# Bias rows copied to DRAM 32 instead of 128 times, read back in four parts, and all loads that are no weights issued by ScalarE or GpSimd

## The chip, the cores and the metric

One core of one Trainium2 chip. The time is the device time of the whole kernel in microseconds (us), the median of several executions.

## What is computed

Two residual networks one after the other, 256 latent tokens (and 256 context tokens) of width 1024, all in float32. `first_block` has four layers, each with an adaLN modulation from `c @ w_ada`: window GQA, MLA, mLSTM, and again a GQA layer. `second_block` takes its result and mixes three branches: NSA heads (a), sliding window heads (b) and forgetting attention (c), then a gated convolutional FFN. What matters here is the relative bias of the a and b heads:

```python
dist = n_prev * Q_BLOCK + qi - ki
bias = jnp.transpose(tab[t5_bucket(dist)], (2, 3, 0, 1))[:, :, None]
logits = jnp.einsum('bgrnqd,bgnkd->bgrnqk', qb, kb).astype(jnp.float32) * (HEAD_DIM ** -0.5) + bias
```

A bias depends on the distance of query and key only. For each head it is one row of 383 values, and a tile of 128 queries by 256 keys needs that row shifted by one for each query.

## The kernel before, in words

Every weight matrix is streamed through a ring of six slots (`w_raw`, NR = 6) of up to 128x1024 float32, 512 KB. SyncE (SP) issues the load of block j + 6 when TensorE has used block j (`w_load`, L3559 to L3564). ScalarE (ACT) rounds a block to its high part (`w_round`, `w_h`), VectorE (DVE) takes the rest (`w_rest`, `w_l`), three blocks ahead of TensorE as a rule, and TensorE does each product in three passes. Every engine takes its instructions strictly in the order in which one shared program emits them; the helper lines L2206 (matmul), L2513 (ACT copy) and L2826 (DVE tensor_tensor) stand for most of them. A `fence` is the newest mark of every engine at that point of the program; whoever waits for it waits for all of them.

All loads that are no weights were also issued by SP in the kernel before, in the same queue as the weight blocks: `gate_load` (a row of gains, one per layer of the first block, L3566), `ml_tables` (L3571), `mix_tables` (six small tables, L3577), `mix_diag` and `mix_bias` (L3589, L3593), `mix_causal` (L3598), `fg_neg` (L3603) and `cp_load` (L3610).

The bias tiles are made in the last layer of the first block (`layer_gqa(3)`, L727 on), by steps of a generator, `Mixers.tables`, placed between its projections. TensorE multiplies a one-hot table with the 32 buckets (`mix_vec_mm`), DVE copies the 8 rows of 384 values to the tile `vec` (`mix_vec`), and `mix_diag` writes `vec` 128 times to a DRAM scratch `[128, 8, 384]`. Both kinds, b and then a, use the one tile `vec`:

```python
    def mix_vec(p, m, b, k):
        p.wait_ge(("mix", "vec_mm", k), ("d_diag", "b") if k == "a" else None)
        p.copy(m.vec[:], p.n.ps[0:8, b, 0:384]).then_inc(*p.mark("mix", "vec", k))
```

Later `mix_bias` reads the scratch back with a row step of one element less than a copy, so that partition p gets the row shifted by p: `BT` `[128, 8, 256]`, 1 MB. BTb is read at the fence in the middle of `layer_gqa(3)`, BTa at the beginning of the b heads' attention.

`layer_gqa` runs the projections q(0) and z(0) (each four blocks and more), then the first attention interleaved with q(1) and z(1), then the second attention interleaved with `ada`, the modulation of the next layer. An attention unit goes PE scores, DVE peak, ACT exponential, DVE scale, PE transpose, ACT copy, PE values.

`fg_neg` writes the forget gate's row to DRAM, waits for that and reads it back as a tile for all partitions; it is emitted between the norms of the c heads' keys, whose power -0.5 runs on GpSimd (POOL, `norm_total`, L3499).

Of the kernel before, what the change touches and what calls it, by code (L numbers as in the profile page):

```python
# [16 lines left out]
D = 1024  # L17
# [153 lines left out]
CONST_AT = {}  # L171
# [56 lines left out]
class Net:  # L228
# [25 lines left out]
    def new(self, name, shape, dt=F32):  # L254
        return self.at(name, shape, dt, self.here(4 * int(np.prod(shape[1:]))))
# [92 lines left out]
def drain(gen):  # L348
    for _ in gen:
        pass  # L350


def weave(main, other, num, den):

    owed = 0
    for _ in main:
        owed += num
        while owed >= den:
            owed -= den
            next(other, None)  # L360
    drain(other)
# [20 lines left out]
def chain(*gens):  # L382
    for g in gens:
        yield from g
# [26 lines left out]
class Steps:  # L411
# [4 lines left out]
    name = None  # L416
# [29 lines left out]
        self.n.value[key] = self.newest = (sem, self.count[key[0]])  # L446
        return sem, 1

    def landed(self, name, *which):

        sem = self.n.sem("_".join([name, *map(str, which)]))
        self.n.value[(name, *which)] = (sem, 16)
        return sem, 16

    def fence(self):
# [10 lines left out]
    gate_load = gate_split = gate_spread = idle  # L466
# [6 lines left out]
    ml_tables = ml_gate_in = ml_sig = ml_scans = ml_ends = ml_max = ml_cols_turn = ml_cols = ml_last_mm = ml_last = idle  # L473
# [3 lines left out]
    mix_tables = mix_gains = mix_vec_mm = mix_vec = mix_diag = mix_bias = norm_in = norm_total = norm_scale = idle  # L477
    mix_dup = mix_key_turn = mix_key_out = mix_v = mix_gz = mix_pos0 = mix_pos_in = mix_pos = mix_causal = idle
    fg_turn = fg_bias = fg_exp = fg_min = fg_scan = fg_neg = fg_col = fg_tanh = fg_gate = idle
    cp_load = cp_hid = cp_hs = cp_turn = cp_g0 = cp_g1 = cp_kv = cp_sq = cp_vc = cp_rs = cp_k = cp_kT = cp_l0 = cp_logits = idle  # L480
# [246 lines left out]
    def layer_gqa(p, i, base, hT, m, mix=None):  # L727

        f = p.fence()
        tables = mix.tables(f) if mix else iter(())  # L730
        next(tables, None)
        drain(m.q(0, hT, f))
        next(tables, None)
        drain(m.z(0, hT, f))
        next(tables, None)
        m.flush()
        p.dense = PAIR
        att = m.attention(0, (0, 1), m.Pt[0], m.PT[0], f, 3, 2)
        steps = 2 * len(m.units(0))
        weave(att, chain(m.q(1, hT, f), m.z(1, hT, f)), 8 * len(m.tiles), steps)  # L740
        m.flush()
        f = p.fence()
        p.stage_tok = [f, f]
        if mix:
            mix.bias("b", f)
        gate, post = p.ends(i, base, 97 if i == 3 else 0, len(m.tiles))
        groups = [(i, 4), (i, 5)] + ([(i + 1, b) for b in range(4)] if i < 3 else [])
        att = m.attention(1, (2, 3), m.Pt[1], m.PT[1], f, 4, 3)
        weave(att, p.ada(PAIR, groups, Gate(p, i, *gate, f), range(5), lag=3), 4 * len(groups) + 2, steps)
        p.dense = DENSE  # L750
        post.free = p.fence()
        return post
# [185 lines left out]
class Weights:  # L938
# [6 lines left out]
    def next(self, name, i, ks, cols, raw=False, ahead=AHEAD):  # L945
        n, b = self.p.n, Block()
        b.j, b.name, b.i, b.words = len(self.order), name, i, ks * cols
        b.is_raw, b.free = raw, None
        b.nsplit = self.split_n
        if not raw:  # L950
            self.split_n += 1
        self.order.append(b)
        s = b.j % NR
        view = lambda t: t[:, 0:ks * cols].rearrange("p (k n) -> p k n", k=ks)
        b.raw, b.h, b.l = view(n.w_raw[s]), view(n.w_h[s]), view(n.w_l[s])
        b.ready = [("loaded", b.j)] if raw else [("w_rounded", b.nsplit), ("w_rest", b.nsplit)]
        self.p.w_load(b.j + NR)
        self.split_to(b.j + ahead, b.j + max(ahead - 1, 0))
        return b
# [849 lines left out]
class Mixers(Later):  # L1809
    def __init__(self, p, base):  # L1810
        n = p.n
# [39 lines left out]
        self.gb, self.tab = new("gains", [128, 6, 64], 1792), new("tab", [33, 16], 3328)  # L1851
        self.oh = {"a": new("oha", [33, 384], 3392), "b": new("ohb", [33, 384], 4928)}
        self.vec = new("vec", [8, 384], 6464)
        self.scr = {k: n.scratch(f"m_bias{k}", (128, 8, 384)) for k in "ba"}
        self.fscr = n.scratch("m_c", (8, 256))
        self.hm, self.sel4, self.row31 = sm[:, 16:24], sm[:, 24:56], sm[:, 56:57]
        self.gz = sm[:, 96:160].rearrange("p (t c) -> p t c", t=2)
# [5 lines left out]
    def tables(self, fence):  # L1863

        p = self.p
        p.mix_tables(self, fence)
        yield
        p.mix_gains(self)
        for x, k in ((1, "b"), (0, "a")):
            b = p.take(TRANS)  # L1870
            p.mix_vec_mm(self, b, x, k)
            p.mix_vec(self, b, k)
            p.give(b, ("mix", "vec", k))
            p.mix_diag(self, k)
            yield

    def bias(self, kind, fence):
        self.p.mix_bias(self, kind, fence)
# [321 lines left out]
class Tensor(Steps):  # L2200


    name = "pe"
# [302 lines left out]
class Scalar(Steps):  # L2506


    name = "act"

    def f(p, out, a, func, bias=0.0, scale=1.0, accum=None):
# [211 lines left out]
    def norm_total(p, m, key, x, nh, a, qs_free, tmp, fence):  # L2723
        p.wait_ge(a, qs_free, fence)
        p.f(m.sq[x][:, 0:nh * 64], m.kn[x][:, 0:nh * 64], ACT.Square).then_inc(*p.mark("norm", "sq", *key))
# [89 lines left out]
    def ff_high(p, m, k):  # L2815
        p.wait_ge(("ffn", "ft", k), m.f)
        p.copy(m.ff.h[:, k, :], m.ft[k % 4][:]).then_inc(*p.mark("ffn", "high", k))


class Vector(Steps):  # L2820


    name = "dve"
# [398 lines left out]
    def mix_tables(p, m, fence):  # L3222
        p.wait_ge(fence)
        p.e.memset(m.tab[32:33, :], NEG).then_inc(*p.mark("mix", "tab"))
# [76 lines left out]
    def fg_neg(p, m, fence):  # L3301
        p.wait_ge(("forget", "c"))
        p.ts(m.f[0][:], m.f[3][:], -1.0, ALU.mult).then_inc(*p.mark("forget", "nc"))
# [42 lines left out]
    def cp_rs(p, m):  # L3346
        st = m.small[0:32, 176:178]
        p.wait_ge(("comp", "sq"))
        p.ts(st[:, 1:2], st[:, 0:1], 1.0 / 64, ALU.mult, EPS, ALU.add).then_inc(*p.mark("comp", "mean"))
# [142 lines left out]
class Pool(Steps):  # L3492


    name = "pool"

    def power(p, out, key, tok):
# [26 lines left out]

    def norm_total(p, m, key, x, nh, a, qs_free, tmp, fence):
        p.power(m.small[:, 64 + 16 * x + 8:64 + 16 * x + 8 + nh], ("norm", "rstd", *key), ("norm", "mean", *key))

    def cp_rs(p, m):
        p.power(m.small[0:32, 177:178], ("comp", "rstd"), ("comp", "mean"))
# [7 lines left out]
class Sync(Steps):  # L3537


    name = "sp"  # L3540
# [18 lines left out]
    def w_load(p, j):  # L3559
        n, s = p.n, j % NR  # L3560
        if j < len(n.order):
            b = n.order[j]
            p.wait_ge(n.order[j - NR].free if j >= NR else None)
            p.e.dma_start(n.w_raw[s][:, 0:b.words], n.w[b.name][b.i]).then_inc(n.sem(f"w_dma{s}"), 16)  # L3564

    def gate_load(p, gate, free):  # L3566
        src = p.n.dram[f"l{gate.i}_g_post"].unsqueeze(0).to_broadcast([128, D])
        p.wait_ge(free)
        p.e.dma_start(gate.gpost[:], src).then_inc(*p.landed("d_gpost", gate.i))

    def ml_tables(p, m, fence):  # L3571
        p.wait_ge(fence)
        for k in ("scan_mul", "scan_add"):
            o = CONST_AT[k][0]
            p.e.dma_start(m.rows[k][:], p.n.dram["cst"][0:64, o:o + 512]).then_inc(*p.landed("d_scan", k))

    def mix_tables(p, m, fence):  # L3577
        n, o = p.n, CONST_AT["hm"][0]
        p.wait_ge(fence)
        p.e.dma_start(m.gb[:].rearrange("p a d -> p (a d)"), n.dram["qk_gain_2"].rearrange("l a d -> l (a d)").to_broadcast(  # L3580
            [128, 384])).then_inc(*p.landed("d_gb"))
        p.e.dma_start(m.small[:, 0:8], n.dram["sinks_2"].to_broadcast([128, 8])).then_inc(*p.landed("d_sinks"))
        p.e.dma_start(m.small[:, 16:57], n.dram["cst"][:, o:o + 41]).then_inc(*p.landed("d_hm"))
        p.e.dma_start(m.tab[0:32, :], n.dram["rel_bias_2"]).then_inc(*p.landed("d_tab"))
        for k, name in (("a", "oh_nsa"), ("b", "oh_swa")):
            o = CONST_AT[name][0]
            p.e.dma_start(m.oh[k][:], n.dram["cst"][0:33, o:o + 384]).then_inc(*p.landed("d_oh", k))

    def mix_diag(p, m, k):  # L3589
        p.wait_ge(("mix", "vec", k))  # L3590
        p.e.dma_start(m.scr[k].rearrange("p h m -> h p m"), m.vec[:].unsqueeze(1).to_broadcast([8, 128, 384])).then_inc(*p.landed("d_diag", k))

    def mix_bias(p, m, k, fence):  # L3593
        src = bass.AP(tensor=m.scr[k].tensor, offset=127, ap=[[8 * 384 - 1, 128], [384, 8], [1, 256]])
        p.wait_ge(("d_diag", k), fence)
        p.e.dma_start(m.BT[k][:], src).then_inc(*p.landed("d_bias", k))

    def mix_causal(p, m, fence):  # L3598
        o = CONST_AT["causal"][0]
        p.wait_ge(fence)  # L3600
        p.e.dma_start(m.causal[:], p.n.dram["cst"][:, o:o + 256]).then_inc(*p.landed("d_causal"))

    def fg_neg(p, m, fence):  # L3603
        p.wait_ge(("forget", "nc"))
        p.e.dma_start(m.fscr, m.f[0][:]).then_inc(*p.landed("d_c"))
        p.wait_ge(("d_c",), fence)
        p.e.dma_start(m.cbc[:].rearrange("p h t -> p (h t)"), m.fscr.rearrange("h t -> (h t)").unsqueeze(0).to_broadcast(
            [128, 2048])).then_inc(*p.landed("d_cbc"))

    def cp_load(p, m, fence):  # L3610
        p.wait_ge(fence)
        p.e.dma_start(m.w2[:], p.n.dram["cmp_w2_2"].rearrange("l w (c p) d -> p (l w) c d", p=128)).then_inc(*p.landed("d_w2"))

    def program(p):
        Steps.program(p)
# [70 lines left out]
```

## Time and profile before

| | us |
|---|---|
| median of three runs | 1620.43 |
| the three runs | 1619.82, 1620.43, 1622.74 |
| the profiled execution | 1617.48 |
| its span, first to last instruction | 1615.7 |
| mean granted TensorE clock over the span | 0.975 |
| busy: PE, DVE, ACT, POOL | 1487.1, 1002.2, 768.4, 67.1 |
| HBM written | 4.20 MB |

The profile is of one execution. Its span is 1.8 us shorter than its time. DMA rows give a transfer by its two tensors, and "SPq" or "ACTq" for the queue that issued it; times are us from the span's start. TensorE's busy time is modelled from its pipelined instructions. The clock is a share of full speed (2.4 GHz): 0.50 is 1.2 GHz.

### The profile page before, as it was taken

The page shows a single profiled execution, that of the slowest core. Times are in us where ns is not written, and L with a number is a line of the kernel's source. Part 1 is how long each engine was busy: PE and PEld are TensorE (multiplying, and loading weights), DVE is VectorE, ACT ScalarE, POOL GpSimd, SP SyncE. Part 2 cuts the span into 40 slices and gives each one's busy share as a digit, 9 for nine tenths or more (in the row PEclk, how much of TensorE's full clock was granted, in tenths as well). Part 3 has the DMA queues.
Part 4 walks back from the last instruction along what each step waited for, and adds up shares of the span by engine and source line. Part 5 has one row for each costly group of instructions (what it writes and reads, how often), then busy time and mean ns, then how long its engine had stood idle before and what let it go on. Part 6 is the DMA issues. An engine that isn't in the chain of part 4 may idle for free.

```text
span 1615.7 us, 24203 instructions
## 1 busy us (share of the span) xinstructions
PE 1487.1 (92%) x9392; PEld 1209.8 (75%) x9392; DVE 1002.2 (62%) x2306; ACT 768.4 (48%) x1642; POOL 67.1 (4%) x74
## 2 busy tenths in 40 slices
PE   6999998999999999999979954988899999989999
PEld 4777756777778787888757743766788889889987
DVE  3547676565566657536585634685776658677763
ACT  4336575453654534321243513574666537455542
POOL 0000000100000100010010000000200110000000
PEclk9999999999999999999989987999899999999999
DMA  9131172321551332211642265233445463345553
GB/s 350 53 105 53 53 260 67 99 91 53 176 190 40 105 111 79 91 53 52 222 157 78 87 119 102 86 124 111 157 143 183 135 221 105 133 157 193 184 190 136
DMA packets 61554, 206.25 MB, mean 128 GB/s; under 512 B 7602, under 2 KB 12412, under 8 KB 61312
## 3 DMA queue, kind: packets, MB, share of 16 engines
q1 hardware_dynamic: 60136, 203.13, 37.9%
q8 instruction: 75, 1.23, 0.3%
q10 hardware_dynamic: 1304, 1.57, 0.3%
q14 instruction: 39, 0.32, 0.1%
HBM read 200.47 MB, written 4.20 MB: 127 GB/s over the span
## 4 chain that ended last, share of the span: by engine, by line
PE 70%; DVE 14%; DMA 7%; ACT 5%; issue 3%; POOL 1%; SPq 0%; POOLq 0%; ACTq 0%; DVEq 0%
PE ps L2206 65%; PE ps L2209 5%; DVE w_l L2826 3%; DMA w_raw<-in_l_q 2%; DMA w_raw<-in_l_z 2%; DMA w_raw<-in_l_out 1%; DVE st L2922 1%; ACT w_h L2513 1%; DVE x L2834 1%; ACT l_P L2516 1%; DVE l_h_lat L2834 1%; DMA w_l_ada<-in_l_ada 1%; DVE m_P L3406 1%; DVE l_P L2830 1%; DVE l_xn L2830 1%
## 5 line engine op out<-in xcount | busy, mean ns | idle before, releaser
L2826 DVE TENSOR_TENSOR w_l<-w_raw,w_h 128x1024 fp32r<-128x1024 f32 (+3 forms) x265 | 316.9, 1206 | 74.5 <-ACT w_h L2513 74.0
L2513 ACT ACTIVATE w_h<-w_raw 128x1024 fp32r<-128x1024 f32 (+3 forms) x265 | 273.3, 1042 | 152.7 <-DMA w_raw<-in_l_q 30.4
L2206 PE MATMUL ps<-w_h,l_hTh 128*128 128x512 f32 (+1 forms) x384 | 157.5, 410 | 0.6 <-DVE w_l L2826 0.5
L2206 PE MATMUL ps<-w_l,l_hTh 128*128 128x512 f32 (+1 forms) x384 | 152.9, 398 | 0.0
L2206 PE MATMUL ps<-w_h,l_hTl 128*128 128x512 f32 (+1 forms) x384 | 152.9, 398 | 0.0
L2516 ACT ACTIVATE l_P<-ps,st 128x512 f32<-128x512 f32 (+1 forms) x128 | 77.6, 608 | 79.6 <-DVE st L2834 52.2
L2206 PE MATMUL ps<-f_hTh,w_h 128*128 128x256 f32 x352 | 99.0, 281 | 0.0
L2206 PE MATMUL ps<-f_hTl,w_h 128*128 128x256 f32 x352 | 98.8, 281 | 0.0
L2206 PE MATMUL ps<-f_hTh,w_l 128*128 128x256 f32 x352 | 98.7, 280 | 0.0
L2206 PE MATMUL ps<-l_hTh,w_h 128*128 128x512 f32 (+1 forms) x264 | 97.4, 369 | 0.5 <-issue 0.5
L2922 DVE TENSOR_REDUCE st<-ps 128x1 f32<-128x512 f32 (+2 forms) x112 | 72.7, 649 | 39.9 <-PE ps L2206 39.4
L2206 PE MATMUL ps<-l_hTl,w_h 128*128 128x512 f32 (+1 forms) x264 | 96.9, 367 | 0.0
L2206 PE MATMUL ps<-l_hTh,w_l 128*128 128x512 f32 (+1 forms) x264 | 96.8, 367 | 0.0
L2206 PEld LDWEIGHTS ps<-w_h,l_hTl 128*128 128x128 f32 x384 | 73.4, 191 | 16.9
L2206 PEld LDWEIGHTS ps<-w_h,l_hTh 128*128 128x128 f32 x384 | 73.6, 192 | 15.6 <-issue 1.4
L2206 PEld LDWEIGHTS ps<-w_l,l_hTh 128*128 128x128 f32 x384 | 73.7, 192 | 14.7
L2206 PE MATMUL ps<-l_PT,l_V 128*64 128x128 f32 (+1 forms) x712 | 70.1, 282 | 3.1 <-DVE l_ogf L2834 3.1
L2206 PEld LDWEIGHTS ps<-l_PT,l_V 128*64 128x64 f32 (+1 forms) x712 | 55.7, 151 | 21.5 <-issue 13.6
L2209 PE MATMUL ps<-cst,l_P 128*128 128x128 f32 x416 | 66.9, 281 | 4.4 <-ACT l_PT L2513 1.7
L2206 PE MATMUL ps<-m_hTh,w_h 128*128 128x256 f32 x224 | 64.8, 290 | 4.1 <-issue 1.3
L2206 PEld LDWEIGHTS ps<-f_hTh,w_h 128*128 128x128 f32 x352 | 66.8, 190 | 0.2 <-issue 0.2
L2206 PEld LDWEIGHTS ps<-f_hTl,w_h 128*128 128x128 f32 x352 | 66.9, 190 | 0.0
(441 smaller groups left out, 3503.1 us busy)
## 6 DMA issues: line engine op xcount, KB each, us to landing
w_raw<-in_l_ada SPq DMA_DIRECT2D x81, 512.0 KB, 4.3
w_raw<-in_l_z SPq DMA_DIRECT2D x32, 512.0 KB, 3.6
w_raw<-in_l_out SPq DMA_DIRECT2D x32, 512.0 KB, 3.6
w_raw<-in_m_merge SPq DMA_DIRECT2D x24, 512.0 KB, 3.3
w_raw<-in_f_gate SPq DMA_DIRECT2D x22, 512.0 KB, 3.2
w_raw<-in_f_up SPq DMA_DIRECT2D x22, 512.0 KB, 3.3
w_raw<-in_f_down SPq DMA_DIRECT2D x22, 512.0 KB, 4.2
w_raw<-in_l_q SPq DMA_DIRECT2D x16, 512.0 KB, 4.6
```

The lines of the kernel that those rows point to most:

```text
L2206: return p.e.matmul(out, lhsT, rhs, start=start, stop=stop)
L2209: return p.e.transpose(out, a, ident)
L2513: return p.e.activation(out, a, func, scale=scale)
L2516: return p.e.activation(out, a, func, bias=bias, scale=scale, accum_out=accum)
L2826: return p.e.tensor_tensor(out, a, b, op)
L2830: return p.e.tensor_scalar(out, a, s1, None, op0)
L2834: return p.e.scalar_tensor_tensor(out, a, s, b, op0, op1)
L2922: p.e.reduce_max(soft.stat(u, 0, nh), ps if nh == 1 else ps.rearrange("p (h k) -> p h k", h=nh), AX.X).then_inc(*p.mark(*soft.key("peak", u)))
L3406: v = p.e.tensor_tensor_reduce(dst, src, bias[i], 1.0, -3.0e38, ALU.add, ALU.max, mx[:, i:i + 1])
```

## The change

The scratch holds 32 copies of the rows in place of 128. `mix_bias` reads it in four loads of 32 partitions each, with the offset lowered by 32 elements per part; they share one semaphore, which is waited for at 64. `gate_load`, `ml_tables`, `mix_tables`, `mix_diag`, `mix_bias`, `mix_causal` and `cp_load` go, otherwise unchanged, from the class of SP to that of ACT, `fg_neg` to that of POOL. In `Mixers.tables` the `yield` stands ahead of `mix_diag` and not behind it, and `layer_gqa` takes one step more from it, so that each copy is issued one step later: copy b after z(0), directly ahead of `mix_vec("a")`, and copy a right behind the flush that follows.

```diff
-    def landed(self, name, *which):
+    def landed(self, name, *which, of=1):
         sem = self.n.sem("_".join([name, *map(str, which)]))
-        self.n.value[(name, *which)] = (sem, 16)
+        self.n.value[(name, *which)] = (sem, 16 * of)
         return sem, 16
...
         next(tables, None)
         m.flush()
+        next(tables, None)
         p.dense = PAIR
...
-        self.scr = {k: n.scratch(f"m_bias{k}", (128, 8, 384)) for k in "ba"}
+        self.scr = {k: n.scratch(f"m_bias{k}", (32, 8, 384)) for k in "ba"}
...
             p.give(b, ("mix", "vec", k))
+            yield
             p.mix_diag(self, k)
-            yield
...
 class Scalar(Steps):
...
+    def gate_load(p, gate, free):
...
+    def ml_tables(p, m, fence):
...
+    def mix_tables(p, m, fence):
...
+    def mix_diag(p, m, k):
+        p.wait_ge(("mix", "vec", k))
+        p.e.dma_start(m.scr[k].rearrange("p h m -> h p m"), m.vec[:].unsqueeze(1).to_broadcast([8, 32, 384])).then_inc(*p.landed("d_diag", k))
+
+    def mix_bias(p, m, k, fence):
+        p.wait_ge(("d_diag", k), fence)
+        for r in range(4):
+            src = bass.AP(tensor=m.scr[k].tensor, offset=127 - 32 * r, ap=[[8 * 384 - 1, 32], [384, 8], [1, 256]])
+            p.e.dma_start(m.BT[k][32 * r:32 * r + 32], src).then_inc(*p.landed("d_bias", k, of=4))
+
+    def mix_causal(p, m, fence):
...
+    def cp_load(p, m, fence):
...
 class Pool(Steps):
...
+    def fg_neg(p, m, fence):
+        p.wait_ge(("forget", "nc"))
+        p.e.dma_start(m.fscr, m.f[0][:]).then_inc(*p.landed("d_c"))
+        p.wait_ge(("d_c",), fence)
+        p.e.dma_start(m.cbc[:].rearrange("p h t -> p (h t)"), m.fscr.rearrange("h t -> (h t)").unsqueeze(0).to_broadcast(
+            [128, 2048])).then_inc(*p.landed("d_cbc"))
...
 class Sync(Steps):
...
-    def mix_diag(p, m, k):
-        p.wait_ge(("mix", "vec", k))
-        p.e.dma_start(m.scr[k].rearrange("p h m -> h p m"), m.vec[:].unsqueeze(1).to_broadcast([8, 128, 384])).then_inc(*p.landed("d_diag", k))
-
-    def mix_bias(p, m, k, fence):
-        src = bass.AP(tensor=m.scr[k].tensor, offset=127, ap=[[8 * 384 - 1, 128], [384, 8], [1, 256]])
-        p.wait_ge(("d_diag", k), fence)
-        p.e.dma_start(m.BT[k][:], src).then_inc(*p.landed("d_bias", k))
```

The other functions are taken out of `Sync` in the same words in which they stand in `Scalar` and `Pool`.

## Rows read from the trace of the kernel before

**Rows 1.** The page: busy us (share of the span) xinstructions.
```profile
PE 1487.1 (92%) x9392; PEld 1209.8 (75%) x9392; DVE 1002.2 (62%) x2306; ACT 768.4 (48%) x1642; POOL 67.1 (4%) x74
```

**Rows 2.** The chain that ended last, by time: start us, us, what.
```profile
...
937.26 33.62 DMA w_raw<-in_l_q
974.80 3.95 PE ps L2206 x9
...
979.19 1.99 PE ps L2206 x9
...
983.63 23.65 DMA w_raw<-in_l_z
```

**Rows 3.** Timeline of SP: start us, us, queue, line, transfer (count).
```profile
936.86 0.31 SPq L3591 DMA_DIRECT2D m_biasb<-m_vec  x1
937.26 13.00 SPq L3564 DMA_DIRECT2D w_raw<-in_l_q  x2
...
973.18 0.30 SPq L3591 DMA_DIRECT2D m_biasa<-m_vec  x1
```

**Rows 4.** Windows: stretch, length, busy us of five engines, TensorE clock, DMA share, GB/s.
```profile
937.00:969.00 32.00, 14.29 (x102) 12.15 (x101) 5.79 (x8) 3.65 (x6) 0.00 (x0) 0.78 0.56 83
969.00:973.00 4.00, 0.00 (x0) 0.00 (x0) 0.73 (x2) 1.33 (x2) 0.00 (x0) 0.50 0.52 208
```

**Rows 5.** Timeline of PE: start us, us, operation, idle before and releaser.
```profile
946.09 0.28 PE L2206 MATMUL ps<-l_hTh,w_l 128*128 128x256 f32 x1
...
974.80 0.80 PE L2206 MATMUL ps<-l_kTh,l_qT 128*128 128x512 f32 x1 [23.52 <-ACT l_P L2516]
...
1008.89 0.75 PE L2209 MATMUL ps<-identr,l_qs 128*128 128x128 f32 x4 [17.57 <-ACT l_PTs L2513]
```

**Rows 6.** Timelines of ACT (four lines) and DVE (one), same columns.
```profile
943.61 0.39 ACT L2515 ACTIVATE l_zT<-ps 128x256 f32<-128x256 f32 x1 [1.47 <-PE ps L2206]
...
970.91 1.06 ACT L2513 ACTIVATE w_h<-w_raw 128x1024 fp32r<-128x1024 f32 x1 [26.91 <-DMA w_raw<-in_l_q]
...
991.24 0.28 ACT L2515 ACTIVATE st<-st,l_sink 128x1 f32<-128x1 f32 x1
1007.30 1.06 ACT L2513 ACTIVATE w_h<-w_raw 128x1024 fp32r<-128x1024 f32 x1 [15.78 <-DMA w_raw<-in_l_z]
...
972.61 0.54 DVE L2837 COPY m_vec<-ps 8x384 f32<-8x384 f32 x1
```

**Rows 7.** The page, DMA issues: count, KB, median us from issue to landing.
```profile
w_raw<-in_l_z SPq DMA_DIRECT2D x32, 512.0 KB, 3.6
```

**Rows 8.** Timeline of all engines at the start of layer_gqa(3).
```profile
922.61 1.04 ACT L2513 ACTIVATE w_h<-w_raw 128x1024 fp32r<-128x1024 f32 x1
922.73 0.69 DVE L2826 TENSOR_TENSOR l_qs<-l_ropeA,l_qs 128x512 fp32r<-128x512 f32 x1 [1.02 <-ACT l_qs L2513]
...
923.49 0.33 SPq L3580 DMA_DIRECT2D m_gains<-in_qk_gain  x1
```

**Rows 9.** Timelines of SP (two lines) and ACT at the second attention's start.
```profile
1046.32 0.38 SPq L3596 DMA_DIRECT2D m_BTb<-m_biasb  x1
1046.74 0.58 SPq L3569 DMA_DIRECT2D l_gpost<-in_l_g_post  x1
...
1047.06 0.69 ACT L2516 ACTIVATE l_P<-ps,st 128x512 f32<-128x512 f32 x1 [1.16 <-DVE st L2834]
```

**Rows 10.** Timelines of SP, POOL, DVE and PE around the forget gate.
```profile
1160.70 0.30 SPq L3605 DMA_DIRECT2D m_c<-m_f  x1
1162.01 0.33 SPq L3607 DMA_DIRECT2D m_cbc<-m_c  x1
...
1161.63 2.54 POOL L3499 TENSOR_TENSOR m_small<-m_small,phalf 128x8 f32<-128x8 f32 x1 [6.09 <-DVE m_small L2831]
...
1167.36 1.23 DVE L2826 TENSOR_TENSOR m_qsl<-m_kn,m_qsl 128x1024 fp32r<-128x1024 f32 x1
...
1172.51 0.81 PE L2209 MATMUL ps<-identr,m_qsl 128*128 128x128 f32 x8
```

More of the change, by code:

```diff
@@ L2817, in ff_high @@
         p.copy(m.ff.h[:, k, :], m.ft[k % 4][:]).then_inc(*p.mark("ffn", "high", k))
+    def gate_load(p, gate, free):
+        src = p.n.dram[f"l{gate.i}_g_post"].unsqueeze(0).to_broadcast([128, D])
+        p.wait_ge(free)
+        p.e.dma_start(gate.gpost[:], src).then_inc(*p.landed("d_gpost", gate.i))
+    def ml_tables(p, m, fence):
+        p.wait_ge(fence)
+        for k in ("scan_mul", "scan_add"):
+            o = CONST_AT[k][0]
+            p.e.dma_start(m.rows[k][:], p.n.dram["cst"][0:64, o:o + 512]).then_inc(*p.landed("d_scan", k))
+    def mix_tables(p, m, fence):
+        n, o = p.n, CONST_AT["hm"][0]
+        p.wait_ge(fence)
+        p.e.dma_start(m.gb[:].rearrange("p a d -> p (a d)"), n.dram["qk_gain_2"].rearrange("l a d -> l (a d)").to_broadcast(
+            [128, 384])).then_inc(*p.landed("d_gb"))
+        p.e.dma_start(m.small[:, 0:8], n.dram["sinks_2"].to_broadcast([128, 8])).then_inc(*p.landed("d_sinks"))
+        p.e.dma_start(m.small[:, 16:57], n.dram["cst"][:, o:o + 41]).then_inc(*p.landed("d_hm"))
+        p.e.dma_start(m.tab[0:32, :], n.dram["rel_bias_2"]).then_inc(*p.landed("d_tab"))
+        for k, name in (("a", "oh_nsa"), ("b", "oh_swa")):
+            o = CONST_AT[name][0]
+            p.e.dma_start(m.oh[k][:], n.dram["cst"][0:33, o:o + 384]).then_inc(*p.landed("d_oh", k))
+    def mix_diag(p, m, k):
[7 more added lines that the diff above has]
+    def mix_causal(p, m, fence):
+        o = CONST_AT["causal"][0]
+        p.wait_ge(fence)
+        p.e.dma_start(m.causal[:], p.n.dram["cst"][:, o:o + 256]).then_inc(*p.landed("d_causal"))
+    def cp_load(p, m, fence):
+        p.wait_ge(fence)
+        p.e.dma_start(m.w2[:], p.n.dram["cmp_w2_2"].rearrange("l w (c p) d -> p (l w) c d", p=128)).then_inc(*p.landed("d_w2"))
 class Vector(Steps):
@@ L3564, in w_load @@
             p.e.dma_start(n.w_raw[s][:, 0:b.words], n.w[b.name][b.i]).then_inc(n.sem(f"w_dma{s}"), 16)
[L3566 to L3587, printed above, removed]
@@ L3589, in mix_diag @@
-    def mix_diag(p, m, k):
-        p.wait_ge(("mix", "vec", k))
-        p.e.dma_start(m.scr[k].rearrange("p h m -> h p m"), m.vec[:].unsqueeze(1).to_broadcast([8, 128, 384])).then_inc(*p.landed("d_diag", k))
-    def mix_bias(p, m, k, fence):
-        src = bass.AP(tensor=m.scr[k].tensor, offset=127, ap=[[8 * 384 - 1, 128], [384, 8], [1, 256]])
-        p.wait_ge(("d_diag", k), fence)
-        p.e.dma_start(m.BT[k][:], src).then_inc(*p.landed("d_bias", k))
[L3598 to L3612, printed above, removed]
```

## The prediction

> **What bounds the kernel now.** I read the page first. TensorE is busy for 92% of the span [rows 1], so only the 8% in which it stands still can be won by moving transfers. The chain of waits in order of time shows where: two of its DMA pieces, in the last attention layer, stand far above the landing time of a block (3.6 us [rows 7]): 33.62 and 23.65 us [rows 2]. Both are loads of a weight block, and both were issued behind a copy of a bias row to DRAM: m_biasb at 936.86, m_biasa at 973.18 [rows 3]. The reader should see three things there.
>
> First, the copy is slow and wide in time, not in bytes. From 937 to 969 the windows show 83 GB/s at a DMA share of 0.56, with weight blocks in between; in the window behind it the blocks left over run at 208 GB/s at a share of 0.52 [rows 4]. So the copy ends at about 969, and a block that needs 3.6 us elsewhere [rows 7] needs 33.6 behind it. Second, TensorE pays for it with 23.52 and 17.57 us of idleness [rows 5], after which it runs at half clock: nine matmuls take 3.95 us, and a little later 1.99 [rows 2]. Third, who is late. ACT waited 26.91 and 15.78 us for the blocks, because it takes its work in order [rows 6]. DVE is late for a second reason: mix_vec("a") overwrites the tile that copy b reads, so it waits until copy b has landed, and it runs at 972.61, just behind the end of copy b [rows 6].
>
> **The change, part by part.** The sum is made against the profiled execution, 1617.48 us, 2.95 below the median of the three runs (1620.43); I take the difference over to the median.
>
> **1. Copies a quarter as long.** The scratch shrinks from 128 to 32 copies, from 1.57 to 0.39 MB each. The outermost dimension stays the 8 heads, so I take the same rate: 969.0 less 937.9 (issue plus about 1 us) is 31.1 us, a quarter of it 7.8. Issue and completion: a block of 512 KB lands in 3.6 us [rows 7], of which its 256 KB on half of the engines at 208 GB/s [rows 4] are 1.3; the other 2.3 I add. A copy alone then takes 10.1 us. Bounds: 3.6, a whole block's landing, if the rate was set by something that the size removes; 34 us, as now, if it doesn't shrink.
>
> **2. Copy b is issued later and loses its cover.** The moved yield puts mix_diag("b") behind all of z(0), directly ahead of mix_vec("a"), which waits for it. Before, the whole of z(0) lay between. Now: z(0)'s last matmul starts at 946.09 [rows 5], its evacuation on ACT takes 0.39 [rows 6], so ACT issues copy b at 946.8. It lands at 946.8 + 10.1 + 1.3 (one weight block shares its engines) = 958.2. Until then DVE stands, and with it the softmax, then TensorE. Behind mix_vec now come 974.80 less 972.61, 2.2 us, until TensorE resumes [rows 5, 6]. It resumes at 960.4 in place of 974.80: **14.4 us won**, not 23.5. Queued behind the wait on DVE are the first reductions and w_l blocks; ACT waits in mix_diag("a") for the same moment, which costs nothing more, as its softmax needs DVE first.
>
> **3. Copy a.** It starts at about 959 and is over at 970. The block that ended the second stall was issued 8.8 us after TensorE resumed (983.63 less 974.80 [rows 2]); now that is 969, and on another queue. So it lands in 3.6 us, before ACT wants it: ACT's step at 1007.30 moves to the end of the one before it, 991.24 + 0.28 = 991.5 [rows 6]: 15.8 us. Without that stall the half clock behind it goes as well, 3.95 less 1.99 = 2.0 [rows 2]. **17.8 us won.** The half clock behind the first stall stays, since TensorE still stands for 9 us.
>
> **4. The six loads of mix_tables on ACT.** SP issued them from 923.49 on, when DVE's l_qs of 922.73 to 923.42 had met the fence [rows 8]. In ACT's order they stand ahead of the rounding now at 922.61. That waits for the fence (0.8) and six issues of 0.33 to 0.43, so it slips by 3.4 us. ACT can catch up later, but DVE's rest of that block stands ahead of the rope of q. I take 2.0 lost (bounds 0 and 3.4).
>
> **5. BTb in four parts and gpost on ACT.** SP issued one load and gpost at 1046.32 and 1046.74, 0.38 and 0.58 us [rows 9]; ACT now issues 4 x 0.38 + 0.58 = 2.1 us from 1046.3 on, and its softmax, on the chain at 1047.06 [rows 9], starts at 1048.4: 1.3 lost (bounds 0 and 2.1). The data are read only in the b heads' attention, a stage later. BTa's four parts (1.5 us by the same 0.38) come while TensorE works through projections that don't need ACT's softmax: nothing, 1.5 without that cover.
>
> **6. fg_neg on POOL.** POOL waits for the forget row, issues m_c, waits for it, issues m_cbc; SP's issues stood at 1160.70 and 1162.01. The power of ck's second tile, at 1161.63 for 2.54 us, is behind them now. DVE's m_qsl ends at 1168.6 and TensorE wants it at 1172.51 [rows 10]: 3.9 us of slack. No row has a DMA issued by POOL. Lower bound SP's 0.3 us each, upper bound that power's 2.54 each: the power ends 1 to 7 us later. I take 0.3 lost (bounds 0 and 3).
>
> **7. The rest** (gpost of layers 0 to 2, scan tables, causal mask, w2): one or two issues of 0.3 to 0.6 us each, in gaps where ACT waits for the same fence or for TensorE. 0.4 lost (0 and 2). SP loses its waits for the bias rows; no block was due in them.
>
> Sum: 14.4 + 17.8 - 2.0 - 1.3 - 0.3 - 0.4 = **28.2 us won**: 1589.3 for the profiled execution, **1592.2** for the median.
>
> **Rivals.** *Copies don't shrink with their bytes.* For: 49 GB/s (1.57 MB in 32 us) is far under what the same engines do, so the limit isn't known. If a copy takes 20 us, DVE stands 10 longer: 1602. Against: the rate is steady over the whole stretch.
>
> *The later copy b turns the gain round.* This is the slower side: DVE's wait for copy b at about 947 is uncovered, each microsecond of it counts. It eats all 28.2 when copy b takes 11.4 + 28.2 = 39.6 us from its issue; at 45 us the time is 1626. This needs a copy that stays at 31 us and is slowed by a third by weights that now interleave with it. Against: the quarter size.
>
> *POOL's issues are slow.* A POOL operation on 128x8 takes 2.54 us beside a busy DVE [rows 10]. At the upper bound TensorE waits 3 us more at 1172, and with the upper bounds of 4 and 5 the time is 1598. The Trainium skill, SBUF — State Buffer, section "SBUF: two separate sides", says that VectorE and GpSimd share a port pair under an exclusive lock, so that descriptors of a DMA issued from GpSimd can wait for a VectorE instruction. By that rule the move to POOL is the wrong way round for this load, and the 3 us are due; no row here shows a DMA of POOL, so the trace neither confirms nor denies it.
>
> *Copy b is short.* If it needs 3.6 us, TensorE hardly stops, and the half clock goes too: 7 and 2 us more, less part of the costs: 1584.
>
> **Chances.** Forecast 0.68; copies shrink less 0.12; POOL and ACT dear 0.10; copy b short 0.07; slower 0.03. A measurement of this kernel can tell about 0.2%, 3.2 us, from no change; only the slow case comes near it (0.01 of "same" is its near edge). The range takes in the short copy and the 20 us copy: 1584 to 1603.
>
> **What would show it.** Right: no DMA piece over 6 us in the chain between 937 and 1010; HBM written falls by 2.4 MB; one idleness of TensorE of 8 to 11 us ended by DVE behind m_vec, at half clock after it; none of 17 us; four loads of BTb on ACTq, softmax behind them about 1.3 us late. Wrong: TensorE's idleness before the softmax over 15 us or under 4; a weight block behind copy a that takes over 8 us; a gap of TensorE at ck's transposes; ACT's roundings at the start of the layer later by more than 4 us.

## The result, and the profile after

| | before | after | ratio, 95% interval |
|---|---|---|---|
| median, us (range) | 1620.12 (1619.43 to 1622.74) | **1596.38** (1592.49 to 1598.45) | 0.9849 [0.9831, 0.9867] |
| profiled execution, us; its span | 1617.48; 1615.7 | 1595.08; 1593.3 | |
| mean granted clock of TensorE in it | 0.975 | 0.981 | |

The change wins 23.7 us, where 28.2 had been worked out; the time lies inside the predicted range (1584 to 1603), 4.2 us above the forecast of 1592.2. The same kernel, timed again beside the experiments, gave 1599.05. The page of the kernel after: the time TensorE is busy, and what the copies write.

```profile
PE 1492.8 (94%) x9392; PEld 1212.9 (76%) x9392; DVE 1002.5 (63%) x2306; ACT 768.8 (48%) x1642; POOL 67.7 (4%) x76
...
HBM read 200.47 MB, written 1.84 MB: 127 GB/s over the span
```

The instructions are the same 9392 matmuls as in [rows 1]; HBM writes fell from 4.20 MB to 1.84, by twice the 1.18 MB that a copy has lost. The chain of waits of after, in order of time, answers to [rows 2]:

```profile
927.96 1.07 ACT w_h L2515
929.05 1.23 DVE w_l L2870
...
934.40 0.85 PE ps L2210 x8
935.25 9.71 PE ps L2207 x44
944.96 0.65 PE ps L2210 x8
945.61 7.09 PE ps L2207 x60
952.73 9.35 DMA m_biasb<-m_vec
...
964.38 4.02 PE ps L2207 x9
...
969.25 2.45 PE ps L2207 x9
...
983.52 0.64 PE ps L2210 x4
984.16 3.88 PE ps L2207 x22
```

Both pieces of a weight block (33.62 and 23.65 us) are gone. In their place stands one new piece, the copy b itself: the kernel no longer waits for weights behind a copy, it waits for the copy. The windows show what the clock did around it (stretch, length, busy us of PE, PEld, DVE, ACT and POOL, TensorE's granted clock, DMA share, GB/s):

```profile
936.00:943.00 7.00, 7.00 (x27) 4.97 (x26) 4.56 (x9) 1.69 (x2) 0.00 (x0) 0.51 0.31 110
943.00:957.00 14.00, 14.00 (x104) 12.32 (x103) 5.78 (x8) 4.99 (x8) 0.00 (x0) 1.00 0.50 160
957.00:964.00 7.00, 0.58 (x3) 0.14 (x1) 1.79 (x4) 0.45 (x1) 0.00 (x0) 0.70 0.33 44
964.00:974.00 10.00, 9.62 (x36) 7.31 (x37) 8.74 (x21) 7.59 (x18) 0.00 (x0) 0.69 0.34 39
974.00:984.00 10.00, 8.18 (x59) 6.09 (x57) 8.14 (x23) 5.89 (x16) 0.00 (x0) 0.99 0.46 157
984.00:988.00 4.00, 4.00 (x25) 2.79 (x23) 2.57 (x6) 2.26 (x5) 0.00 (x0) 0.60 0.08 10
```

The row of 957 to 964 is the stall; the first, the fourth and the last are stretches at half clock (1.2 GHz), wholly or partly. Before, TensorE had a clock of 1.00 from 925 to 940. The timeline has the three idle times of PE in front of them (three rows), and DVE's row names the copy as what held the first softmax back; [rows 5, 6] are the rows of before:

```profile
934.40 0.85 PE L2210 MATMUL ps<-identr,l_qs 128*128 128x128 f32 x8 [1.74 <-DVE l_qs L2870]
964.38 0.79 PE L2207 MATMUL ps<-l_kTh,l_qT 128*128 128x512 f32 x1 [6.79 <-ACT l_P L2518]
983.52 0.64 PE L2210 MATMUL ps<-identr,l_qs 128*128 128x128 f32 x4 [1.67 <-ACT l_PTs L2515]
962.18 0.55 DVE L2881 COPY m_vec<-ps 8x384 f32<-8x384 f32 x1 [8.61 <-DMA m_biasb<-m_vec]
```

Now the first 1.74. ACT's timeline at the start of layer_gqa(3) has the six table loads between two roundings:

```profile
923.88 0.61 ACT L2515 ACTIVATE l_qs<-l_ropeA 128x512 fp32r<-128x512 f32 x1
925.30 0.33 ACTq L2835 DMA_DIRECT2D m_gains<-in_qk_gain  x1
...
927.54 0.37 ACTq L2842 DMA_DIRECT2D m_ohb<-in_cst  x1
927.96 2.01 ACT L2515 ACTIVATE w_h<-w_raw 128x1024 fp32r<-128x1024 f32 x2 [3.47 <-issue]
```

To see where time is won and lost I took the start of the same ACT instruction in both traces and subtracted. The kernel after comes into the last attention layer 1.8 us late, stands 6.3 us late behind the tables, 10.4 early behind the first softmax, 9.5 early ahead of the place of the old second stall, 25.3 behind it, 22.9 behind the start of the second attention, and 22.4 early at the end. The first 1.8 is a drift that differs from run to run (the repeat of the same kernel has 0.8 at that point).

### The profile page after: what moved, and what is told of

Read it like the earlier page. It is cut to its first block, busy times and chain, and to the rows that moved or that the text cites. A ratio compares the mean times of both kernels' runs of the same rounds, so it can differ in the third digit from the quotient of the medians.

```text
span 1593.3 us, 24198 instructions
## 1 busy us (share of the span) xinstructions
PE 1492.8 (94%) x9392; PEld 1212.9 (76%) x9392; DVE 1002.5 (63%) x2306; ACT 768.8 (48%) x1642; POOL 67.7 (4%) x76
## 3 DMA queue, kind: packets, MB, share of 16 engines
HBM read 200.47 MB, written 1.84 MB: 127 GB/s over the span
## 4 chain that ended last, share of the span: by engine, by line
PE 73%; DVE 14%; ACT 5%; DMA 4%; issue 3%; POOL 1%; ACTq 0%; SPq 0%; POOLq 0%; DVEq 0%
PE ps L2207 67%; PE ps L2210 5%; DVE w_l L2870 3%; DVE st L2966 1%; DMA w_raw<-in_l_out 1%; DVE x L2878 1%; ACT l_P L2518 1%; ACT w_h L2515 1%; DMA w_l_ada<-in_l_ada 1%; DVE l_h_lat L2878 1%; DMA m_biasb<-m_vec 1%; DVE l_xn L2874 1%; DVE l_P L2874 1%; DMA w_raw<-in_m_aq 1%; POOL mstat L3544 0%
## 5 line engine op out<-in xcount | busy, mean ns | idle before, releaser
L2207 PEld LDWEIGHTS ps<-w_l,l_hTh 128*128 128x128 f32 x384 | 73.5, 192 | 14.8
```

Of the source, the lines that this page charges most:

```text
L2207: return p.e.matmul(out, lhsT, rhs, start=start, stop=stop)
```

## The experiments

All were timed against the kernel before, which was timed again with each of the three batches (1620.27, 1620.99 and 1620.74). The ratios carry an interval of about 0.2 to 0.25%, 3 to 4 us, so small steps are read from the traces. A trace shows one execution only: differences between two traces that lie away from the edited place are scatter, and they reach several us. The "distance" given below is how far the same ACT instruction starts behind (+) the fastest kernel found (32 copies, all on SP but the two copies themselves).

### First batch: size alone, and two parts undone

**The kernel after again** gives the reference for the others.

> The changed kernel once more, as the measure for the others of this set. Both theories: 1596, within 0.2%.

1599.05 us, ratio 0.987 [0.9848, 0.9891]. The trace repeats that of after row for row: chain piece of copy b 9.36 us, TensorE's half clock at 935 and at 984.

**Size alone**, the kernel before with

```
-        self.scr = {k: n.scratch(f"m_bias{k}", (128, 8, 384)) for k in "ba"}
+        self.scr = {k: n.scratch(f"m_bias{k}", (32, 8, 384)) for k in "ba"}
...
-        ... m.vec[:].unsqueeze(1).to_broadcast([8, 128, 384])
+        ... m.vec[:].unsqueeze(1).to_broadcast([8, 32, 384])
```

and the four reads, every transfer and the yield where they were.

> The kernel before with 32 copies and four reads, everything still issued by SP and at its old place. Theory (the length of the copies is the whole gain, the move of the queue only costs): copy b lands at about 947, ahead of mix_vec a, and the weight blocks behind either copy are at most 8 us late, most of which the blocks in hand cover; both idle times of TensorE go and no load is added to ACT: 1580 to 1584. Rival (the weight blocks must leave the copies' queue): blocks behind each copy still stall TensorE for 5 to 8 us each, so that it is no faster than the changed kernel: 1592 to 1598.

**1581.98 us**, ratio 0.9766 [0.9747, 0.9786]. The theory held: size alone wins 38 us, and the rest of the change costs 14 to 17 (1596.38 or 1599.05 less 1581.98). The four reads came in with the smaller size, but the first of them is issued at 1011.35, behind both places where TensorE had stood, so they can't be what removed these stalls. The timelines of SP and DVE in this kernel show why nothing waits for the row: DVE writes it again at 953.94, 12.1 us behind the issue of copy b and without a wait, with the whole of z(0) between them.

```profile
941.85 0.31 SPq L3591 DMA_DIRECT2D m_biasb<-m_vec  x1
942.24 3.92 SPq L3564 DMA_DIRECT2D w_raw<-in_l_q  x2
948.55 3.13 SPq L3564 DMA_DIRECT2D w_raw<-in_l_z  x2
954.51 0.30 SPq L3591 DMA_DIRECT2D m_biasa<-m_vec  x1
...
953.94 0.54 DVE L2837 COPY m_vec<-ps 8x384 f32<-8x384 f32 x1
```

**mix_tables back on SP**, otherwise the kernel after.

```
 class Scalar(Steps):
-    def mix_tables(p, m, fence):
...
 class Sync(Steps):
+    def mix_tables(p, m, fence):
```

> The changed kernel with mix_tables back on SP. Theory (the six issues on ACT delay the rounding and DVE's rest, TensorE waits 1.7 us and then runs 7 us at half clock, 4.5 us in all): 1592, and no idle time of TensorE ahead of the transposes of q. Rival (the 4.5 us are covered later, or are scatter of the two profiled executions): 1596.

1588.77 us, ratio 0.982 [0.9793, 0.9847]: 7.6 to 10.3 us better than after by the medians, more than expected, with five runs from 1585.67 to 1594.51. Copy b's piece is still 9.37 us and TensorE still stands 6.79. What is gone is the half clock ahead of it, a part of that behind it, and all of it at the place that follows (22 matmuls in 2.49 us against 3.88). The windows of this kernel:

```profile
925.00:940.00 15.00, 14.58 (x92) 12.21 (x93) 12.96 (x21) 6.23 (x9) 0.00 (x0) 1.00 0.59 192
...
958.00:968.00 10.00, 10.00 (x44) 7.69 (x45) 9.57 (x24) 8.34 (x19) 0.00 (x0) 0.83 0.35 43
...
976.00:980.00 4.00, 3.93 (x33) 3.06 (x34) 3.10 (x8) 2.90 (x8) 0.00 (x0) 1.00 0.15 40
```

Behind the same stall of 6.79 us the next ten microseconds have a clock of 0.83 here and 0.69 in the kernel after. In the traces the kernel after loses 4.7 us against this one ahead of the copy, about 1 behind the stall and about 1.5 at the 22 matmuls, some 7 in all. The 1.5 can't be put down to the tables: other kernels below have the half clock at that place with the tables on SP.

**The yield back**, otherwise the kernel after.

```
             p.give(b, ("mix", "vec", k))
+            p.mix_diag(self, k)
             yield
-            p.mix_diag(self, k)
```

and the extra `next(tables, None)` out.

> The changed kernel with the yield behind mix_diag again and one step less in layer_gqa: copy b is issued by ACT right behind mix_vec b, ahead of z(0). Theory (the wait of mix_vec a for the later copy b is what is left of the first stall): copy b is issued at about 941, lands at 951, mix_vec a waits for at most 1 us, TensorE loses neither the 7 us nor the half clock behind them: 1587. Rival (ACT's wait for mix_vec b, or the copy beside the blocks of z, takes it back): 1594 to 1598.

1583.72 us, ratio 0.9772 [0.9751, 0.9793]: 12.7 to 15.3 better than after by the medians, 10.1 by the two traces. Here ACT issues copy b at 940.94 and copy a at 954.32. The 9.4 us of the copy lie inside these 13.4, and TensorE has one idle time over 1 us from 936 to 975, 1.68 at its end.

### Second batch: the queue alone, the yield alone

**128 copies in the kernel after**, the first line of the size edit taken back.

> The changed kernel with 128 copies of each row again (the four reads take the first 32): queue moves and later copies, without the smaller size. Theory (the later copy b is paid for by its whole length): copy b goes out at about 953 as in the changed kernel, lasts about 32 to 34 us, the second DVE write of the row waits for it, so PE stands some 23 us longer there than in the changed kernel, and nothing waits behind copy a: 1616 to 1630, no better than the kernel before. Rival (the second rival of the prediction, that queue moves win the second stall and the late copy costs nothing): about 1602.

1630.18 us, ratio 1.0056 [1.0034, 1.0078]: slower than before, and just above the theory's range; the rival (1602) fell. The theory was right on the first stall (23.7 us longer than in the kernel after) and wrong in that nothing would wait behind copy a. TensorE's timeline:

```profile
991.38 0.79 PE L2207 MATMUL ps<-l_kTh,l_qT 128*128 128x512 f32 x1 [30.50 <-ACT l_P L2518]
...
1020.58 0.75 PE L2210 MATMUL ps<-identr,l_qs 128*128 128x128 f32 x4 [11.77 <-ACT l_PTs L2515]
```

The first stall is longer than the 23.52 of [rows 5], because the copy starts later; the second is still there, shorter than the 17.57 of before, though copy and weights stand in two queues.

**The two copies alone to ACT**, 128 of them, in the kernel before (mix_diag moved from Sync to Scalar).

> The kernel before with the two copies of 128 rows issued by ACT instead of SP, nothing else. Theory (both stalls of before come from the length of the copy, the first by the row buffer, the second by the queue): the weight loads no longer stand behind the copies, PE's first idleness shrinks to what the buffer alone asks (copy b out at about 937 to 941, done 32 us later, 14 to 20 us idle instead of 23.5), the second of 17.6 us is gone: 1594 to 1604. Rival (the copies hold the weight loads back by using the same DMA engines, in whatever queue): both stalls stay, 1612 to 1622.

1613.68 us, ratio 0.9947 [0.9928, 0.9966]: my theory (1594 to 1604) failed, and the time lies in the rival's range. Three rows of its chain:

```profile
939.93 34.32 DMA m_biasb<-m_vec
...
985.95 17.82 DMA w_raw<-in_l_z
1006.13 3.72 PE ps L2206 x22
```

A block needs 17.82 us on SP's queue while a copy runs from ACT's. So a long copy slows the weights whatever queue it is in. The queue isn't without effect at this length: the block issued right behind copy b lands after 17.14 us here and after 33.62 in one queue with it, and TensorE's second idleness is 11.73 us in place of 17.57. But the first stays at 21.94 (23.52 before), since DVE's second write still waits for the copy itself. The queue by itself is worth about 7 us of the 38 (5.5 to 11.7 by the interval of the ratio).

**The yield alone**: size alone, as above, with the yield moved and the extra `next(tables, None)`, all on SP.

> The best one so far (kernel before with 32 copies and four reads, all issued by SP) with the yield moved ahead of the copy and the one more step of the tables, as in the changed kernel. Theory (it is the moved yield that delays copy b by some 12 us, whichever engine issues it): copy b goes out at about 950 to 955, the second write of the row waits for it, PE stands 5 to 8 us and gets the half clock after: 1589 to 1597. Rival (the delay came from ACT's order of work, not from the yield): 1580 to 1584.

1586.14 us, ratio 0.9778 [0.9755, 0.98]: between the two by its median, and 4.2 us above size alone, which the intervals don't tell apart. The trace decides for the theory's mechanism: copy b goes out at 954.72, 10.4 us behind its row (944.3), the second write waits 9.0 us for it, and TensorE's timeline has

```profile
966.41 0.80 PE L2207 MATMUL ps<-l_kTh,l_qT 128*128 128x512 f32 x1 [7.18 <-ACT l_P L2517]
```

The distance grows from 7.0 ahead of this place to 14.8 behind it, 7.8 us. So it is the yield that delays the copy, on either engine. How much of the 7.8 us the whole time keeps on SP is less sure: the execution in the trace is the slowest of the five (1591.53).

**The copies alone to ACT**, 32 of them, at their old places.

> Kernel before with 32 copies and four reads, the two copies alone issued by ACT at their old places, everything else by SP. Theory (with copies of 9.4 us the queue they stand in hardly matters): the weight block no longer waits 10 us behind copy b, ACT is held back once by up to 1 us: 1578 to 1583, within 2 us of the same with SP. Rival (ACT's place in the queue costs by itself, because ACT waits for the row before it can go on): 1584 or more.

**1579.38 us**, ratio 0.9748 [0.9726, 0.9771], the fastest found, though not told apart from 1581.98. The reason I gave was wrong. I had expected the weight block not to wait behind copy b; its chain has

```profile
937.70 9.99 DMA w_raw<-in_l_q
```

and with the copy on SP's queue the same piece is 9.98 us. For copies of this length the queue makes no difference to the weights.

### Third batch: the other parts, one at a time on the fastest kernel

**Six table loads to ACT.**

> The best one so far (kernel before, 32 copies, four reads, the two copies alone on ACT) plus the six table loads of layer_gqa(3) on ACT: part 4 of the prediction by itself. Theory (they push ACT's rounding of a weight back, PE stands 1.7 us and then has the half clock for some 7 us): slower than the best one by 3 to 5 us, 1582 to 1585. Rival (the forecast's own term, ACT's time alone): slower by 2.0 us or less, 1579 to 1581.5.

1585.01 us, ratio 0.9767 [0.9746, 0.9789], 5.6 slower than without them by the medians and 3.1 by the ratios, whose intervals overlap. The trace shows the step: the distance grows from 0.5 at 915 us to 4.9 at 938, and from 950 on it is 3.9, so 3.4 of the 4.4 us stay. TensorE's timeline has one gap, and then the windows of this kernel and of the one without the edit differ:

```profile
933.94 0.85 PE L2209 MATMUL ps<-identr,l_qs 128*128 128x128 f32 x8 [1.93 <-DVE l_qs L2842]
```

From 930 to 945 us the granted clock is 0.77 with the loads on ACT, 1.00 without.

**Eight reads of the bias rows and gate_load to ACT.**

> The same best one plus the eight reads of the bias rows and all gate_load on ACT: part 5 by itself. Theory (offset of 2.6 us seen behind 1020 us in the changed kernel): slower by 2.5 us, 1581 to 1583. Rival (the forecast's 1.3 us): 1580 to 1581. The loads of layers 0 to 2 should show nothing.

1581.00 us, ratio 0.9765 [0.9739, 0.979]; the medians can't tell 1.3 from 2.5. The distance steps from 3.9 to 6.5 at this place, 2.6. In this trace most of it is gone again by 1100 us (4.4), while in the kernel after at most 0.9 is; so 2.6 is the loss on the spot, and what stays in the end is not settled. In the kernel after, the rows are ACT's (three) and PE's (one):

```profile
1020.84 1.81 ACTq L2852 DMA_DIRECT2D m_BTb<-m_biasb  x4
1022.68 0.48 ACTq L2824 DMA_DIRECT2D l_gpost<-in_l_g_post  x1
1023.21 0.69 ACT L2518 ACTIVATE l_P<-ps,st 128x512 f32<-128x512 f32 x1 [2.80 <-DVE st L2878]
1024.04 0.50 PE L2207 MATMUL ps<-l_kTh,l_qT 128*128 128x512 f32 x1 [2.36 <-ACT l_P L2518]
```

The softmax is 1.66 us late (3.12 us behind the last l_qT, 1.46 with the loads on SP). TensorE stands 2.36 us in place of 0.71, and then has a clock of 0.59 from 1024 to 1028, where the fastest kernel has 1.00.

**fg_neg to GpSimd.**

> The same best one plus fg_neg's two transfers issued by GpSimd: part 6 by itself. Theory (hidden, 0.3 us): 1578 to 1581. Rival (descriptor making by GpSimd delays its power operations and those delay VectorE at the transposes of ck): slower by 3 us or more, 1583 and above.

1581.85 us, ratio 0.9757 [0.9738, 0.9775]. The distance is 1.3 us ahead of this place and 1.2 behind it: hidden. The rows of GpSimd in the kernel after:

```profile
1137.47 0.74 POOL L3575 DMA_DIRECT2D m_c<-m_f  x1 [5.44 <-DVE m_small L2881]
1140.23 0.58 POOL L3577 DMA_DIRECT2D m_cbc<-m_c  x1 [2.02 <-DMA m_c<-m_f]
1140.82 1.67 POOL L3544 TENSOR_TENSOR m_small<-m_small,phalf 128x8 f32<-128x8 f32 x1
```

From the first issue to the second 2.76 us pass here, and 1.31 with SP [rows 10]: the detour over GpSimd is slower, but nothing waits for it.

**16 copies, read back in eight parts.**

> The same best one with 16 instead of 32 copies, read back in eight parts by SP. Theory (the copy of 9.4 us is hidden already, only the weights beside it come a little sooner, and eight reads cost SP 1.8 us more): within 1.5 us of 32 copies, 1578 to 1581. Rival (the transfer is still in the way at 9.4 us): 1572 to 1576. If each copy's time goes with its size, it lasts about 5 us.

1581.50 us, ratio 0.9753 [0.9731, 0.9775]: nothing won. The block beside copy b is on the chain no longer, and at the last of z(0) this kernel is 2.6 us ahead; by the first softmax 0.7 of that is left, and behind the next gap of TensorE nothing (clock 0.91 from 960 to 980, against 1.00). How long this copy lasted isn't in its trace as a wait, so the 5 us stay open; the block beside it landed after 6.70 us, where it took 9.99 beside 32 copies.

## Why the prediction held, and where it was off

**What bounds the kernel** held: size alone takes both stalls away. But I divided the cause wrongly. I read the 33.62 us of [rows 2] as a block behind a copy in one queue and let the new queue carry a part of the second win. The runs with 128 copies on ACT's queue show that the queue takes a block from 33.62 to 17.14 us, but TensorE's stalls only from 23.52 and 17.57 to 21.94 and 11.73; with 32 copies the pieces are equal (9.98 and 9.99). The length of the copy is nearly all, and shrinking it alone would have won 38 us where the forecast for the whole change was 28.2.

**Part 1**, a copy in 10.1 us, 11.4 with a block beside it: measured 9.35 from issue to landing, beside a block. The rate carried over, as assumed.

**Part 2** held in its mechanism and nearly in size. ACT issued copy b behind z(0)'s evacuation at 952.73 (946.8 forecast, plus the 6.3 by which the kernel was late there makes 953.1), and TensorE resumed 2.2 us behind the row, at 964.38, as forecast. The distance to before goes from 6.3 late to 10.4 early: 16.7 won against 14.4, the shorter copy being nearly all of the difference. What this part didn't ask is what the moved yield costs against leaving it: on SP 7.8 us by one trace and 4.2 by the medians, in the kernel after 10.1 by the traces and 12.7 to 15.3 by the medians.

**Part 3**: 15.8 for the stall and 2.0 for the half clock behind it. Across that place the kernel goes from 9.5 early to 25.3, 15.8 us; the ACT rounding stands directly behind the step before it (982.04 behind 981.75 + 0.28). A weight block issued behind copy a (974.16) landed in 3.38 us, as forecast. The 2.0 didn't come: 22 matmuls at 984.16 took 3.88 us. "Without that stall the half clock behind it goes as well" was the failed sentence: a gap of 1.67 us is left there, and it was enough in this kernel, though not in every one (last section). The 2.0 itself was read from the wrong place, the nine matmuls behind the first stall; behind the second the same 22 took 3.89 us before, and 2.49 at full clock, so 1.4 were to be had.

**Part 4 is the term that was mis-sized**: 2.0 with bounds 0 and 3.4, measured 4.5 (1.8 to 6.3), and 4.4 alone, of which 3.4 stayed. ACT slipped 3.47 us, as worked out. The step that failed is that I priced the slip by ACT's time only: it left TensorE 1.74 us idle, and 27 matmuls then took 7 us at half clock. Behind the copy's stall the half clock lasted longer as well, about 1 us. The list of signs had set its mark too high for it: ACT's rounding at 927.96 is 3.5 us late, not over 4.

**Part 5** likewise: 1.3 forecast, 1.66 on ACT, 2.6 on the spot with the half clock behind it (bound 2.1). **Part 6** held: GpSimd's issues take 0.74 and 0.58 us, its power was 1.67 instead of 2.54 and ended 1.9 us later, and the kernel was not delayed. The port lock that the Trainium skill, SBUF — State Buffer, section "SBUF: two separate sides", describes cost nothing that this trace shows. **Part 7**: no loss of its own was found; the drift of up to 4 us in layers 0 to 2 appears as well in the kernel that has all these loads on SP.

Sum: 16.7 - 4.5 - 0.9 (the half clock that lasts to 974) + 15.8 - 2.6 is 24.5, and less the 1.8 of drift at the start, 22.7; 22.4 is measured between the two spans. So the median came out near the forecast partly by luck: copy b was 2 us shorter than worked out, and that paid back about half of what parts 4 and 5 cost beyond their terms.

Of the signs that I had named for a right forecast, HBM's 2.4 MB (2.36), the missing stall of 17 us and the late softmax came. Two were off: I had asked for no DMA piece over 6 us in the chain, though part 2 itself puts copy b there (9.35), and for an idleness of 8 to 11 us, which was 6.79.

**The rivals.** *Copies don't shrink*: fell (9.35 us). *The later copy turns the gain round*: it fell for this change, but its mechanism is real. With 128 copies the change makes the kernel slower by 0.56%: copy b's piece is then 33.08 us, and that was enough, where I had put the break-even at 39.6. Most of the missing part is the second stall, which I took as gone with the queue and which stayed (11.77 us); parts 4 and 5 add to it. *GpSimd and ACT dear*: half true, for ACT alone (its terms add up to 1597.4, not 1598). *Copy b short*: fell by size, though what it described, a copy that hides, is what the old place of the yield gives: not the copy had to be shorter, but its issue earlier.

## What to carry to other kernels

When a small transfer reads a buffer that is written again soon, issue it at the first moment and let work lie between: the same 9.4 us kept nobody waiting when issued at 941, and made DVE wait 8.61 us and TensorE 6.79 at 953. Shrinking a slow transfer beat every choice of its queue here (38 us against 7), so test the parts of such an edit one by one. Price a delay of TensorE's feeder with the half clock that may follow, not by the delay alone, and keep a row of issues (six here) off the engine that feeds it when SP is free.

## What was not expected of the hardware

Short gaps were followed by the half clock in some places and not in others. The gap of 1.74 to 1.93 us ahead of the transposes of q stands in five traces (after, its repeat, the yield back, 128 copies in after, and the table loads alone), and each has the half clock behind it (0.51 for 7 us in the kernel after). So do the five with a gap of 2.35 or 2.36 us ahead of the second attention's softmax matmuls (0.58 to 0.64 over 4 us). But the gap of 1.67 or 1.68 us ahead of l_qs's transposes, which all 11 traces with 32 or 16 copies have, goes both ways. The 22 matmuls behind it took 3.88 us in the kernel after, 3.87 in its repeat, 3.57 with size alone and 3.88 with 16 copies; in the other seven they took 2.49 or 2.50. Rows of size alone, of 16 copies and of the fastest kernel:

```profile
974.99 3.57 PE ps L2206 x22
...
969.54 3.88 PE ps L2206 x22
...
970.23 2.49 PE ps L2206 x22
```

No single part of the change sorts the two groups: the half clock comes with the tables on ACT and on SP, with the yield early and late, with and without a long stall ahead. So two traces can be 1.1 to 1.4 us apart at this place, and no edit made here accounts for it. The Trainium skill, TensorE: Matmul & The Clock Gate, section "What's actually happening", says that the chip judges recent activity at moments that don't follow the kernel; by that rule the same gap can fall either way. The rows agree with that, but no run here moved a gap alone, so the cause stays open.

A copy of 32 rows from ACT's queue slows a weight block on SP's as much as one on SP's own (9.99 and 9.98 us). With 128 copies it doesn't: 17.14 us from the other queue against 33.62 in the same one. What the two queues share was not measured.
